# Residual kept transposed in four PSUM banks, and scatter and gather moved into the middle of the first expert weight's matmuls

## The reference

```python
def moe(x, w_r, b_r, w1, b1, w2, b2):
    ...
    for e in range(N_EXPERTS):
        hdn = xt @ w1[e] + b1[e]
        gate = jnp.minimum(hdn[:, :D_FF_EXPERT], SWIGLU_LIMIT)
        up = jnp.clip(hdn[:, D_FF_EXPERT:], -SWIGLU_LIMIT, SWIGLU_LIMIT)
        act = (up + 1.0) * gate * jax.nn.sigmoid(SWIGLU_ALPHA * gate)
        out = out + combine[:, e:e + 1] * (act @ w2[e] + b2[e])
    return out.reshape(B, T, D)
...
        h = h + moe(rmsnorm(h, g_ffn[l]), w_r[l], b_r[l], w1[l], b1[l], w2[l], b2[l])
        gate = jax.nn.sigmoid(rmsnorm(h, g_ple[l]) @ w_pg[l] + b_pg[l])
        h = h + gate * (p[l] @ w_pp[l])
    return rmsnorm(h, g_final), ...
```

## Time and profile before

| | |
|---|---|
| median of three runs | 1093.55 us (1091.79 to 1093.87) |
| the profiled execution | 1091.18 us |
| its span in the trace | 1089.5 us |
| TensorE busy, share of the span | 1061.2 us, 97% |
| VectorE busy, share of the span | 385.1 us, 35% |
| ScalarE busy, share of the span | 168.2 us, 15% |
| HBM, mean over the span | 391 GB/s |

### The profile page before, as it was taken

The page is one execution under the profiler, slowest core; times in us unless marked ns, Lnnn a source line. Parts: engine busy times, 40 slices in busy tenths (PEclk is TensorE's granted clock), DMA queues, the critical chain, the costliest instruction groups (busy, mean ns, idle before and its releaser), DMA issues.

```text
span 1089.5 us, 13468 instructions
## 1 busy us (share of the span) xinstructions
PE 1061.2 (97%) x5250; PEld 429.7 (39%) x5250; DVE 385.1 (35%) x875; ACT 168.2 (15%) x298; POOL 13.8 (1%) x20
## 2 busy tenths in 40 slices
PE   9999999999999999999999999999999999999996
PEld 7884433444333333333333333333333333333342
DVE  6563743222333333333333333333333332333326
ACT  2550600010000000000000000000000000000034
POOL 0100200000000000000000000000000000000000
PEclk9999999999999999999999999999999999999999
DMA  9957699998999999999999999999999999999941
GB/s 281 354 216 300 262 401 428 424 397 374 395 431 430 433 431 433 430 428 434 427 432 433 426 434 425 432 430 431 431 437 426 434 430 431 433 422 430 423 182 40
DMA packets 34312, 426.80 MB, mean 392 GB/s; under 512 B 5383, under 2 KB 8655, under 8 KB 16493
## 3 DMA queue, kind: packets, MB, share of 16 engines
q1 hardware_dynamic: 34284, 426.41, 93.6%
HBM read 424.57 MB, written 1.43 MB: 391 GB/s over the span
## 4 chain that ended last, share of the span: by engine, by line
PE 76%; DMA 22%; DVE 1%; ACT 0%; SPq 0%; issue 0%; DVEq 0%
PE bank L1669 29%; DMA ring<-in_w 21%; PE bank L1710 17%; PE bank L1344 5%; PE bank L1599 5%; PE bank L1581 3%; PE bank L1432 3%; PE bank L1607 2%; PE bank L1592 2%; PE bank L1689 2%; PE bank L1767 1%; PE bank L1779 1%; DMA w_in<-in_w_in 1%; PE bank L1695 1%; PE bank L1654 1%; PE bank L1534 1%
## 5 line engine op out<-in xcount | busy, mean ns | idle before, releaser
L1669 PE MATMUL bank<-ring,xgT 128*64 128x512 f32 x2048 | 447.5, 593 | 14.5 <-DMA ring<-in_w 14.5
L1669 PEld LDWEIGHTS bank<-ring,xgT 128*64 128x64 f32 x2048 | 145.5, 137 | 298.3 <-issue 267.6
L1710 PE MATMUL bank<-ring,actT 128*64 128x512 f32 x1024 | 233.6, 598 | 0.0
L1177 DVE TENSOR_SCALAR gmin<-bank 128x512 f32<-128x512 f32 x32 | 22.1, 692 | 338.9 <-PE bank L1669 338.9
L1710 PEld LDWEIGHTS bank<-ring,actT 128*64 128x64 f32 x1024 | 67.9, 136 | 141.4 <-issue 120.5
L700 ACT ACTIVATE sig<-gmin 128x512 f32<-128x512 f32 x32 | 20.1, 630 | 446.4 <-DVE gmin L1177 446.4
L1131 DVE TENSOR_TENSOR h<-bank,h 128x512 f32<-128x512 f32 x132 | 84.8, 684 | 8.7 <-PE bank L1599 7.6
L1085 DVE TENSOR_TENSOR xgT<-bank,vecT 128x512 f32<-128x512 f32 x32 | 22.1, 692 | 155.9 <-PE bank L1592 155.2
L1171 DVE TENSOR_SCALAR wpick<-slot_no,pos,share 128x128 f32<-128x128 f32 (+1 forms) x96 | 27.1, 339 | 112.5 <-PE bank L1669 112.5
L1599 PE MATMUL bank<-y,wpickT 64*128 64x512 f32 x264 | 65.6, 615 | 0.8 <-ACT y L711 0.8
L711 ACT ACTIVATE y<-bank 128x512 f32<-128x512 f32 x32 | 19.1, 597 | 237.5 <-PE bank L1710 237.5
(11 more groups left out here) (306 smaller groups left out, 645.6 us busy)
## 6 DMA issues: line engine op xcount, KB each, us to landing
ring<-in_w SPq DMA_DIRECT2D x53, 4096.0 KB, 32.0
ring<-in_w SPq DMA_DIRECT2D x86, 2048.0 KB, 28.4
w_in<-in_w_in SPq DMA_DIRECT2D x3, 2048.0 KB, 14.2
w_out<-in_w_out SPq DMA_DIRECT2D x1, 4096.0 KB, 17.0
w_pg<-in_w_pg SPq DMA_DIRECT2D x4, 1024.0 KB, 26.7
h<-in_x_prompt SPq DMA_DIRECT2D x2, 512.0 KB, 3.9
w_in<-in_w_in SPq DMA_DIRECT2D x2, 512.0 KB, 7.8
w_in<-in_w_in SPq DMA_DIRECT2D x1, 1024.0 KB, 10.8
```

What stands on the lines that cost most here:

```text
L1669: ins = pe.matmul(bank[part][r, :], xgT[:, (k % FOUR) * W1_QUADS + k // FOUR, :], w[:, c:c + HALF], start=False, stop=(k == W1_SLOTS - 1), ...
L1710: ins = pe.matmul(bank[2][CAP * m:CAP * (m + 1), :], actT[:, half:half + CAP], pair[:, c:c + HALF], start=(f == 0), stop=(f == FF // P - 1 ...
```

## The change

The residual of the 256 prompt positions moves into PSUM: at step 0 TensorE writes `h` transposed (channels on the partitions) into banks 4 to 7 (`residual_in`), and each scatter adds to these banks in place, with `y` as weights and `wpickT` moving. The additions of VectorE (`add_tile`) go. The samples' residual, transposed by `samples_in`, is kept in SBUF as `hT_samples`; the samples' scatter writes to free columns of banks 0 and 2, from which VectorE adds it. From step 1 on, scatter and gather stand after the first weight's fourth chunk instead of after its eighth; step 0 keeps the old place. The embedding is computed transposed, in one piece after step 3. The tail works with channels on the partitions: `w_pg` as weights and 264 tokens moving, biases and gains as columns of `vecT` (two more short loads in place of two rows spread over the partitions), sums over channels by additions on VectorE and small matmuls on TensorE, and transposes back to tokens before the output.

```diff
@@ tensor: the scatter
-            def scatter(t, rows, first_bank):
-
-                for m in range(2):
-                    r = slice(CAP * m, CAP * (m + 1))
-                    ins = pe.matmul(bank[first_bank + m][0:rows, :], wpickT[r, t * P:t * P + rows], y[r, :],
-                                    start=True, stop=True)
-                ins.then_inc(spread, 1)
+            def residual_in():
+
+                for b in range(KD):
+                    for t in range(2):
+                        pe.matmul(residual(b)[:, t * P:(t + 1) * P], h[:, t, b * P:(b + 1) * P], ident[:],
+                                  start=(b % 2 == 0 and t == 0), stop=False, skip_group_check=True)
+
+            def scatter(blocks=range(KD // 2), last=False):
+
+                for c in blocks:
+                    for m in range(2):
+                        r, b = slice(CAP * m, CAP * (m + 1)), KD // 2 * m + c
+                        ins = pe.matmul(residual(b), y[r, c * P:(c + 1) * P], wpickT[r, 0:SEQ], start=False, stop=last,
+                                        skip_group_check=True)
...
+            def scatter_samples(blocks=range(KD // 2)):
+
+                for c in blocks:
+                    for m in range(2):
+                        r = slice(CAP * m, CAP * (m + 1))
+                        at_c = (0 if m else T) + c * NS
+                        ins = pe.matmul(bank[2 * m][:, at_c:at_c + NS], y[r, c * P:(c + 1) * P], wpickT[r, SEQ:T],
+                                        start=True, stop=True, skip_group_check=True)
...
@@ tensor: a step
+                def spread_and_gather():
+
+                    if started:
+                        pe.wait_ge(wpickT_ready, 1)
+                    pe.wait_ge(y_ready, i + 1)
+                    if started:
+                        samples_in()
+                        residual_in()
+                    scatter()
+                    if not (tail and phase == LAST - 1):
+                        gather(i + 1)
+
                 pe.wait_ge(xgT_ready, i + 1)
                 for k in range(W1_SLOTS):
+                    if k == W1_SLOTS // 2 and not started:
+                        spread_and_gather()
...
                 if started:
-                    pe.wait_ge(wpickT_ready, 1)
-                pe.wait_ge(y_ready, i + 1)
-                pe.wait_ge(h_added, i * 2 * NT + NT)
-                scatter(0, P, 4)
-                scatter(1, P, 6)
-                if not (tail and phase == LAST - 1):
-                    gather(i + 1)
+                    spread_and_gather()
 
                 pe.wait_ge(act_ready, i + 1)
...
                 ins.then_inc(wpick_turned, 1)
-                scatter_samples(4)
-
+                scatter_samples()
+
+                pe.wait_ge(h_added, i + NT + 2)
                 pe.wait_ge(actT_ready, i + 1)
...
@@ vector: a step, after the activation
-                add_tile(0, P, 4, i * NT + 1, i * 2 * NT + NT)
-                add_tile(1, P, 6, i * NT + 2, i * 2 * NT + NT + 2)
+                add_samples(i * 2 + 2, i + NT + 1)
                 if not last:
                     make_xgT(i + 1, gathered_turned)
-                add_samples(4, i * NT + 3, i * 2 * NT + NT + 4)
...
@@ tensor: the embedding, and the gate in the tail
+            def embed(b):
+
+                if b > 1:
+                    pe.wait_ge(pw_ready, b - 1)
+                for k in range(PLE // P):
+                    ins = pe.matmul(bank[b % 2][:, 0:T], w_pp[:, b, k, :], pT[:, k, :], start=(k == 0),
+                                    stop=(k == PLE // P - 1))
                 ins.then_inc(pw_made, 1)
...
+                    ins = pe.matmul(bank[GATE_BANKS[b]][:, 0:T], w_pg[:, k, b * P:(b + 1) * P], tail_nT[:, k, :],
+                                    start=(j == 0), stop=(j == KD - 1), skip_group_check=True)
```

More of the change, by code:

```diff
@@ L741, in _ @@
[L741 to L750, removed]
+            for j in range(2):
+                act.wait_ge(spread, n * 2 + 1 + 3 * j)
+                for b in (2 * j, 2 * j + 1):
+                    act.activation(tail_nT[:, b, 0:SEQ], residual(b), ACT.Identity, scale=vcol("g_ple", b)
+                                   ).then_inc(tail_nT_act, 1)
@@ L1123, in _, with add_samples @@
                 make_shares(r)
-            def add_tile(t, rows, first_bank, products, added):
+            samples_wide = hT_samples[:].rearrange("p k s -> p (k s)")
+            def add_samples(products, added):
                 dve.wait_ge(spread, products)
                 dve.wait_ge(h_added, added)
-                for m in range(2):
-                    src = bank[first_bank + m]
-                    dve.tensor_tensor(h[0:rows, t, halves(m)], src[0:rows, :], h[0:rows, t, halves(m)], ALU.add
-                                      ).then_inc(h_added, 1)
@@ new lines, in add_embedded @@
+            def add_embedded(b):
+                dve.wait_ge(plegate_ready, b + 1)
+                link(dve.tensor_tensor(gate[:, b, :], gate[:, b, :], pwT[:, b, :], ALU.mult))
+                dve.tensor_tensor(gate[:, b, SEQ:T], gate[:, b, SEQ:T], hT_samples[:, b, :], ALU.add)
+                dve.tensor_tensor(gate[:, b, 0:SEQ], gate[:, b, 0:SEQ], residual(b), ALU.add).then_inc(h_final, 1)
+            for b in range(KD - 1):
+                normal(b)
+                if b > 0:
+                    add_embedded(b - 1)
@@ L1735, in _ @@
             pe.wait_ge(wpickT_ready, n + 1)
-            pe.wait_ge(h_added, n * 2 * NT + NT)
-            scatter(0, P, 4)
-            scatter(1, P, 6)
-            def turn_four(t, half, dst):
-                for c in range(4):
-                    k = 4 * half + c
-                    ins = pe.transpose(dst[:, c * P:(c + 1) * P], h[:, t, k * P:(k + 1) * P], ident[:])
-                ins.then_inc(tail_turned, 1)
-            pe.wait_ge(h_added, n * 2 * NT + NT + 2)
-            turn_four(0, 0, bank[2])
@@ new lines, in _, with wait_tail, spread_sums @@
+            scatter(range(2), True)
+            pe.wait_ge(y_right_ready, 1)
+            scatter_samples()
+            scatter(range(2, 4), True)
+            def wait_tail(k):
+                if k < KD // 2:
+                    pe.wait_ge(tail_nT_act, k + 1)
+                else:
+                    pe.wait_ge(tail_nT_dve, k - KD // 2 + 2)
+            def spread_sums():
+                pe.wait_ge(sums_ready, 1)
+                ones = group_sum[:, 0:1].to_broadcast([P, P])
+                pe.matmul(bank[3][:, 0:T], ones, token_sums[:, 0, :], start=True, stop=True).then_inc(sums_spread, 1)
```

435 lines of the change are left out of this document (213 added, 222 removed).

## The result

The changed kernel takes **1251.11 us** (median of four runs, 1249.62 to 1251.51) against 1093.71 us (1091.79 to 1094.22) of the kernel before, run beside it: 1.1436 times the time, 95% interval 1.142 to 1.1452. Forecast were 1169 us and a range that ended at 1206. The sign and the waits are as forecast; on top of them comes a loss of TensorE's clock, which the forecast had as a rival with a chance of 0.06.

A forecast was written before the change was run, and what follows sets the result against it. TensorE was taken to bound the kernel, with transfers pacing some steps at 29.2 us. Thirty steps of 30.64 plus 7.8 gave +71.5 us; with +5.3, +1.9 and -1, +77.7 on 1091.18: 1169 us, range 1142 to 1206.

The forecast's parts named there:

- the sum: One step of the expert loop: 27.57 + 2.46 + 0.55 - 0.04 + 0.1 = 30.64 us; steps 1 to 30: 927.0 us.
- the clock: Rival, chance 0.06: TensorE's clock falls to half in the wait before the transposes; 1229 us, up to 1440.
- those 3 us: End of the kernel before: the clock went to half some 3 us after TensorE's work ended, longer than the 2.46 us wait.
- The rival's price: Half clock behind the wait: +2 us a step on the small work (1229), +7 with the whole second weight (1440).
- new wait: TensorE waits before the second weight until VectorE has added the samples' sums: 0.55 us a step, between 0.4 and 0.75.
- The scatter: In the first weight's middle, 8 matmuls of 256 columns for 4 of 512: 1.92 us again, bounds 1.73 and 2.65.
- Back to the first weight: TensorE's return to the first weight's matmuls after the gather: 0.1 us a step, between 0 and 0.19.
- The bounds of the parts: Lower and upper limits of one expert-loop step from its terms' limits: 29.9 to 32.6 us.
- The samples' scatter: Ahead of the second weight, 8 matmuls with `y` as weights, loads in pairs: 0.92 us; unpaired 1.84, lower bound 0.66.
- weights one by one: Rival, chance 0.20: the samples' loads don't pair, or the scatter shows its loads; 31.4 to 32.6 us a step, 1192 to 1228.
- Not slower: Rival, chance 0.05: moved scatter and gather fill the wait for transfers; steps 1 to 30 average under 28.0 us.
- Once only: Costs outside the repeated step: step 0 +5.3 us, step 31 +1.9, embedding after step 3 7.8, tail -1.

The follow-up runs named there:

- the place alone: Kernel before, with only its scatter and gather moved to the middle of the first weight and its additions to `h` ahead of the gate's clamp: 1177.55 us.
- the run with the clock held: Changed kernel plus three fp32 matmuls (512, 512 and 256 columns, result unread) in the wait before the activation's transposes: 1171.79 us.

## Why the prediction was wrong

- **The failed step** is the price of the clock, which the sum put at nothing: the rival "the clock" had 0.06, with the argument "those 3 us are more than the wait". The clock fell in each of steps 1 to 31, and cost 2.7 us a step. The argument failed in two ways. First, the 3 us are one reading, behind the last matmul of the kernel before, taken as fixed. In the step above the fall came 3.3 us after the last wide matmul (426.07 - 2.39 = 423.68, and 426.95), over the steps of the changed kernel between 2.7 and 5.4 us after it, and with the place alone 2.2 us after it, inside the wait. Second, they were held against the wait alone. The transposes, the 8-column matmuls and the second wait prolong the stretch without wide matmuls to 429.53, the second weight's start; they were counted as work, and the run with small matmuls in the wait shows that such work did not keep the clock. Neither sign by which the prediction called itself wrong (transposes that wait less than 1 us, a wait for the ring) would have told this; the clock within a step, its sign for the rival, did.
- **The rival's price** was off too. "The small work behind it would run at half (+2 us a step, 1229)" and "the whole second weight too (+7, 1440)" were its two ends; in the step above it is 33.68 - 30.63 = 3.05 us: 1.58 - 1.06 = 0.52 on the small matmuls and 6.19 - 3.65 = 2.54 on the first half of the second weight. The run lies between the two ends, nearer the lower. Steps 1 to 30 took 1172.42 - 164.73 = 1007.69 us against 927.0 forecast, 80.7 more, or 2.7 a step. With the last step's 2.9, of which 0.56 is that step's own new wait, left out of the sum, and 0.8 less in the tail, this is about the whole miss of 82 us.
- **The warning was right.** The Trainium skill (TensorE: Matmul & The Clock Gate, section HAM oscillation) says that a loop which idles TensorE in each turn can be throttled in each. The trace agrees: the clock is 0.91 over 600 us of the loop, and each step's length is above 32 us. Its example waits longer than here, and for transfers; here it is for VectorE, and the sum without the clock was 30.64.
- **The other terms of the step**, in the run with wide matmuls in the wait, at full clock: from the first weight's end to the transposes 530.03 - 527.57 = 2.46 (2.46 forecast; 2.39 of it shows as idle where nothing fills it). The new wait before the second weight 0.48 (0.55). The scatter 519.07 - 517.14 = 1.93 (1.92), so neither bound. Back to the first weight (0.1): its two halves take 6.97 + 6.96 = 13.93 us against 13.83 in one piece, but the gather is 0.10 shorter in its new place (1.54 against 1.64), which the sum did not have. That 30.63 meets 30.64 so closely is in part luck: the samples' scatter is 0.14 over its term, and the gather and the new wait together 0.17 under theirs. The bounds of the parts add up to 29.8 and 32.7, not 29.9 and 32.6; nothing hangs on it.
- **The samples' scatter** (0.92, paired): 1.06 at full clock, and records of one row half alone take nearly twice as long each, so the rival "weights one by one" falls. By the Trainium skill (TensorE: Matmul & The Clock Gate, section LDWEIGHTS) a load's time goes with its columns and not with its rows. The trace agrees where eight loads use one row half (0.95 us, 0.119 each, against 0.115 at full height); where two halves alternate, 16 in 1.06 us show more than one at a time.
- **Not slower** falls: the waits for the ring are gone, as they would have been, but all of the 2.39 us shows. **Once only**: step 0 took 164.73 - 131.74 = 32.99 us, 5.35 more than before (+5.3 forecast); the embedding made its step 8.0 us longer in the run with the clock held (7.8); from the last second weight to the end it is 45.9 us against 47.7, -1.8 (-1 forecast).

What stays open is what exactly TensorE's clock counts: the order of the runs by wait, by busy time or by the whole stretch without wide matmuls is not the order of their losses, the fall comes at no fixed time after the last wide matmul, and some steps of equal rows lose the clock while others keep it.

The rows on which the lengths of step 0, of steps 1 to 30 and of the end rest, of the changed kernel:

```profile
131.74 0.62 PE L1646 MATMUL bank<-b_parts,b_pick 96*64 96x512 bf16 x4
...
164.73 0.60 PE L1646 MATMUL bank<-b_parts,b_pick 96*64 96x512 bf16 x4
...
1172.42 0.60 PE L1646 MATMUL bank<-b_parts,b_pick 96*64 96x512 bf16 x4
...
1195.23 8.62 PE L1707 MATMUL bank<-ring,actT 128*64 128x512 f32 x32 [0.56 <-DVE hT_samples L1150]
```

## What to carry to other kernels

When a wait on TensorE is uncovered, price the loss of the clock as well, and look at the whole stretch until the next wide matmuls, transposes and weight-load-bound matmuls included. A fall read at another place of the kernel gives no safe length (some 3 us at the end of the kernel before, 2.2 to 5.4 us here), the wait alone is the wrong measure, and busy time does not answer it; the granted clock of a run does. What fills a wait on another engine with wide matmuls is worth its cover and its clock: here scatter and gather were worth 5 us a step, of which the wait that they cover is half. If nothing useful fits, even matmuls whose result nobody reads can pay (1171.79 against 1251.11 us).

## What was not expected of the hardware

- The clock falls while TensorE shows as busy and idles only 0.28 and 0.55 us (second weight's first half 6.13 us).
- Steps with equal work lose the clock in a fixed turn: 30.03 and 31.4 us in alternation with the place alone, a turn of four (32.1, 33.6, 33.7, 33.7) in the changed kernel.
- The fall follows the last wide matmul at no fixed distance: 2.2 us with the place alone, 2.7 to 5.4 us in the changed kernel.
- Weight loads of one fp32 row half, put together, cost nearly twice as much each: 8 records in 0.95 us, against 16 alternated (in halves and banks) in 1.06.
